# Feed-forward weight-quarter sums issued by GpSimd in tile order instead of by VectorE

## What is computed

```python
def swiglu_ffn(x, w_in, w_out):
    gate, up = jnp.split(x @ w_in, 2, axis=-1)
    return (jax.nn.silu(gate) * up) @ w_out

for i in range(DEPTH):            # DEPTH = 2, D_FF = 2816, D_MODEL = 1024
    x = x + 0.5 * swiglu_ffn(rmsnorm(x, norm_g[i, 0]), ffn_w_in[i, 0], ffn_w_out[i, 0])
    ...                           # pooling or convolution mixer
    x = x + 0.5 * swiglu_ffn(rmsnorm(x, norm_g[i, 2]), ffn_w_in[i, 1], ffn_w_out[i, 1])
```

## Time and profile before

| | |
|---|---|
| median of the runs | 2587.79 us |
| span of the profiled execution | 2585.3 us |
| TensorE matmul busy | 2552.6 us, 99% |
| VectorE busy | 1904.1 us, 74% |
| ScalarE busy | 1264.0 us, 49% |
| GpSimd busy | 191.5 us, 7% |
| mean granted TensorE clock | 0.997 |

### The profile page before, as it was taken

One profiled execution on the slowest core, in us unless ns is written; L12 is line 12 of the kernel. 1 busy time (PEld: TensorE's weight loads), 2 busy tenths in 40 slices (PEclk: granted clock), 3 DMA queues, 4 the chain that ended last, 5 costly groups with the idle time before them and its releaser, 6 DMA issues.

```text
span 2585.3 us, 43699 instructions
## 1 busy us (share of the span) xinstructions
PE 2552.6 (99%) x17223; PEld 2171.8 (84%) x17223; DVE 1904.1 (74%) x3109; ACT 1264.0 (49%) x2140; POOL 191.5 (7%) x248
## 2 busy tenths in 40 slices
PE   9999999999999989999999999999999999999999
PEld 7787878887777768999988999989999864889998
DVE  5765655686666678877769777688777698897775
ACT  5544445456665654444454444454444413444444
POOL 1110101013000010000020000010000421100000
PEclk9999999999999999999999999999999999999999
DMA  4222222122222212333322332223323472322232
GB/s 137 84 82 67 82 67 92 40 82 102 81 81 73 73 50 82 107 114 107 99 99 82 115 99 98 99 82 105 108 98 99 127 180 75 98 98 99 98 100 81
DMA packets 171883, 241.78 MB, mean 94 GB/s; under 512 B 6545, under 2 KB 149403, under 8 KB 171443
## 3 DMA queue, kind: packets, MB, share of 16 engines
q1 hardware_dynamic: 164755, 216.27, 25.7%
q0 software_dynamic: 6368, 21.79, 3.0%
q10 hardware_dynamic: 576, 1.16, 0.1%
HBM read 233.54 MB, written 5.58 MB: 92 GB/s over the span
## 4 chain that ended last, share of the span: by engine, by line
PE 88%; DVE 6%; ACT 2%; issue 2%; DMA 1%; POOL 0%; SPq 0%; POOLq 0%; DVEq 0%; ACTq 0%
PE ps L2000 8%; PE ps L2002 8%; PE ps L2001 8%; PE ps L440 5%; PE ps L442 5%; PE ps L441 5%; PE ps L2020 5%; PE ps L2021 5%; PE ps L2022 5%; PE ps L858 5%; PE ps L860 4%; PE ps L859 4%; PE ps L2748 1%; DMA w_raw<-in_ffn_w_out_dram 1%; DVE probs L1814 1%
## 5 line engine op out<-in xcount | busy, mean ns | idle before, releaser
L858 PE MATMUL ps<-h_hi,w_hi 128*128 128x512 f32 x608 | 255.2, 420 | 2.5 <-DVE w_lo L417 1.3
L2020 PE MATMUL ps<-a_hi,w_hi 128*128 128x512 f32 x640 | 250.2, 391 | 4.6 <-DVE a_lo L2315 4.6
L2122 ACT ACTIVATE wg<-w_raw 128x512 fp32r<-128x512 f32 x256 | 153.7, 624 | 197.7 <-PE ps L2002 98.0
L2021 PE MATMUL ps<-a_lo,w_hi 128*128 128x512 f32 x640 | 249.8, 390 | 0.0
L2022 PE MATMUL ps<-a_hi,w_lo 128*128 128x512 f32 x640 | 249.5, 390 | 0.0
L860 PE MATMUL ps<-h_hi,w_lo 128*128 128x512 f32 x608 | 237.9, 391 | 0.0
L859 PE MATMUL ps<-h_lo,w_hi 128*128 128x512 f32 x608 | 237.8, 391 | 0.0
L2000 PE MATMUL ps<-mix_late,wg 128*128 128x256 f32 x832 | 235.2, 283 | 0.1
L2002 PE MATMUL ps<-mix_late,wg 128*128 128x256 f32 x832 | 234.7, 282 | 0.0
L2001 PE MATMUL ps<-mix_late,wg 128*128 128x256 f32 x832 | 234.6, 282 | 0.0
L417 DVE TENSOR_TENSOR w_lo<-w_raw,w_hi 128x2048 fp32r<-128x2048 f32 x90 | 206.1, 2290 | 29.4 <-ACT w_hi L412 29.4
(11 more groups left out here) (463 smaller groups left out, 6614.4 us busy)
## 6 DMA issues: line engine op xcount, KB each, us to landing
w_raw<-in_ffn_w_in_dram SPq DMA_DIRECT2D x88, 1024.0 KB, 5.1
w_raw<-in_ffn_w_out_dram SPq DMA_DIRECT2D x44, 1024.0 KB, 4.9
w_raw<-in_a_w_in_dram SPq DMA_DIRECT2D x24, 1024.0 KB, 5.4
w_raw<-in_b_w_in_dram SPq DMA_DIRECT2D x16, 1024.0 KB, 5.4
w_raw<-in_conv_w_pw_dram SPq DMA_DIRECT2D x12, 1024.0 KB, 5.9
shifted<-glu_scratch POOLq DMA_DIRECT2D x32, 264.0 KB, 7.5
w_raw<-in_a_w_out_dram SPq DMA_DIRECT2D x8, 1024.0 KB, 4.9
w_raw<-in_b_w_out_dram SPq DMA_DIRECT2D x8, 1024.0 KB, 4.9
```

What stands on the lines that cost most here:

```text
L858: nc.tensor.matmul(dst, wh[:, w], h_hi[:, k], start=k == 0, stop=False)
L2020: nc.tensor.matmul(dst, wh[:, w], a_hi[:, buf, k], start=h == 0 and k == 0, stop=False, skip_group_check=h == 1)
L2021: nc.tensor.matmul(dst, wh[:, w], a_lo[:, buf, k], start=False, stop=False, skip_group_check=h == 1)
```

## The change

The four sums of every mixed gate and up tile are issued by GpSimd. `quarter_sum` calls `nc.gpsimd.tensor_tensor`, all its calls are taken out of `dve_steps` and `dve_ff`, and a new `gp_ff` issues them tile by tile, 5, 6, 7, 3 in each. `gp_ff` is called after `gp_sums` of each feed-forward's norm and first waits until the norm is broadcast, since the sums use its buffers. The sum of quarter 5 also waits for its own engine's earlier sum 6. Shapes, buffers and values are the same, and so is every other engine's order.

```diff
-        def quarter_sum(dve, f, s, u, *xs):
+        def quarter_sum(pool, f, s, u, *xs):
...
-            tt, t, i = nc.vector.tensor_tensor, step_tile(f, s, u), mixed_before(f, s, u)
+            tt, t, i = nc.gpsimd.tensor_tensor, step_tile(f, s, u), mixed_before(f, s, u)
             for x in xs:
                 if x == 5:
-                    dve.wait_ge(raw_loaded[t % 2], 16 * (t // 2 + 1))
-                    low_before(dve, f, s, u, 5)
+                    pool.wait_ge(raw_loaded[t % 2], 16 * (t // 2 + 1))
+                    low_before(pool, f, s, u, 5)
+                    if i:
+                        pool.wait_ge(mix_sum[6], i)
                     ins = tt(mix_s1, corner(t, 1, 0), corner(t, 1, 1), ALU.add)
                 elif x == 6:
-                    dve.wait_ge(mix_sum[5], i + 1)
-                    low_before(dve, f, s, u, 6)
+                    pool.wait_ge(mix_sum[5], i + 1)
+                    low_before(pool, f, s, u, 6)
                     if i:
-                        dve.wait_ge(mix_sum[3], i)
+                        pool.wait_ge(mix_sum[3], i)
                     ins = tt(mix_s2, mix_s1, corner(t, 0, 0), ALU.subtract)
                 elif x == 7:
-                    dve.wait_ge(mix_sum[5], i + 1)
+                    pool.wait_ge(mix_sum[5], i + 1)
                     ins = tt(corner(t, 1, 0), corner(t, 0, 0), corner(t, 1, 0), ALU.subtract)
                 else:
-                    dve.wait_ge(mix_sum[6], i + 1)
-                    dve.wait_ge(mix_lo, quarters_before(f, s, u, 2) + 1)
+                    pool.wait_ge(mix_sum[6], i + 1)
+                    pool.wait_ge(mix_lo, quarters_before(f, s, u, 2) + 1)
                     ins = tt(corner(t, 0, 1), corner(t, 0, 1), mix_s2, ALU.subtract)
                 ins.then_inc(mix_sum[x], 1)
+
+        def gp_ff(pool, f, m):
+
+            pool.wait_ge(bcast_ready, SPREAD.index(m) + 1)
+            for s in range(PLAIN, FF_STEPS):
+                for u in "gu":
+                    quarter_sum(pool, f, s, u, 5, 6, 7, 3)
...
         def dve_steps(dve, f, r):
             a, b = 2 * r + 1, 2 * r + 2
             add_pair(dve, f, r - 1, 5)
-            quarter_sum(dve, f, b, "g", 5)
             quarter_low(dve, f, a, "u", 2)
-            quarter_sum(dve, f, a, "u", 3)
-            quarter_sum(dve, f, b, "g", 6, 7)
...
             gp_sums(pool, 2)
+            gp_ff(pool, 0, 2)
             pool.wait_ge(band_stored, 16)
...
             gp_sums(pool, 4)
+            gp_ff(pool, 1, 4)
             gp_sums(pool, 5)
+            gp_ff(pool, 2, 5)
...
             gp_sums(pool, 8)
+            gp_ff(pool, 3, 8)
```

More of the change, by code:

```diff
@@ L2333, in add_pair, with low_before @@
                 nc.vector.scalar_tensor_tensor(xT[:, n], ps[:, 4 + n % 4], 0.5, xT[:, n], ALU.mult, ALU.add).then_inc(out_free, 1)
-        def low_before(dve, f, s, u, x):
+        def low_before(pool, f, s, u, x):
             i = mixed_before(f, s, u)
             if i:
-                dve.wait_ge(mix_lo, 7 * (i - 1) + MIX.index(x) + 1)
-        def quarter_sum(dve, f, s, u, *xs):
+                pool.wait_ge(mix_lo, 7 * (i - 1) + MIX.index(x) + 1)
+        def quarter_sum(pool, f, s, u, *xs):
@@ L2425, in dve_steps @@
             quarter_low(dve, f, b, "g", 5)
-            quarter_sum(dve, f, b, "u", 5, 7)
             quarter_low(dve, f, b, "g", 6, 2)
-            quarter_sum(dve, f, b, "g", 3)
             join(dve, f, a, "u", "c11")
-            quarter_sum(dve, f, b, "u", 6)
             quarter_low(dve, f, b, "g", 3)
@@ L2441, in dve_steps @@
             low_half(dve, f, a, 1)
-            quarter_sum(dve, f, b, "u", 3)
             join(dve, f, b, "g", "c11")
@@ L2456, in dve_steps @@
             low_half(dve, f, b, 0)
-            quarter_sum(dve, f, a + 2, "g", 5)
             low_half(dve, f, b, 1)
             quarter_low(dve, f, a + 2, "g", 1, 5)
-            quarter_sum(dve, f, a + 2, "g", 6)
             add_pair(dve, f, r, 0)
@@ L2465, in dve_steps @@
             add_pair(dve, f, r, 2)
-            quarter_sum(dve, f, a + 2, "g", 3)
             add_pair(dve, f, r, 3)
-            quarter_sum(dve, f, a + 2, "g", 7)
             quarter_low(dve, f, a + 2, "g", 3)
-            quarter_sum(dve, f, a + 2, "u", 5)
             quarter_low(dve, f, a + 2, "g", 7, 4)
             quarter_low(dve, f, a + 2, "u", 1, 5)
-            quarter_sum(dve, f, a + 2, "u", 6, 7)
             add_pair(dve, f, r, 4)
@@ L2506, in dve_ff @@
             hs_sum(dve, f, 6)
-            quarter_sum(dve, f, 2, "g", 5)
             ff_product(dve, f, 1, 1)
@@ L2512, in dve_ff @@
             add_first(dve, f, 1, 2)
-            quarter_sum(dve, f, 2, "g", 6)
             add_first(dve, f, 3)
@@ L2519, in dve_ff @@
             hs_low(dve, f, 3)
-            quarter_sum(dve, f, 2, "g", 3, 7)
             hs_low(dve, f, 7)
             quarter_low(dve, f, 2, "g", 3, 7, 4)
-            quarter_sum(dve, f, 2, "u", 5)
             quarter_low(dve, f, 2, "u", 1)
             join(dve, f, 2, "g", "c11")
-            quarter_sum(dve, f, 2, "u", 6)
             quarter_low(dve, f, 2, "u", 5)
@@ L2534, in dve_ff @@
             low_half(dve, f, 1, 1)
-            quarter_sum(dve, f, 2, "u", 3, 7)
             split_out(dve, f, 1)
@@ L2550, in dve_ff @@
             low_half(dve, f, 2, 1)
-            quarter_sum(dve, f, 3, "g", 5)
             quarter_low(dve, f, 3, "g", 1, 5)
             add_pair(dve, f, 0, 0, 1)
-            quarter_sum(dve, f, 3, "g", 6)
             add_pair(dve, f, 0, 2)
-            quarter_sum(dve, f, 3, "g", 7)
             add_pair(dve, f, 0, 3)
             quarter_low(dve, f, 3, "g", 6, 2)
-            quarter_sum(dve, f, 3, "g", 3)
-            quarter_sum(dve, f, 3, "u", 5, 6)
             quarter_low(dve, f, 3, "g", 3, 7, 4)
             quarter_low(dve, f, 3, "u", 1, 5, 6)
-            quarter_sum(dve, f, 3, "u", 7)
             add_pair(dve, f, 0, 4)
```

## The result

The changed kernel takes 2616.9 us in the median (2614.53 to 2618.84) against 2587.51 us of the kernel before in the same session: a ratio of 1.0112, with a 95% interval of 1.0098 to 1.0126. The forecast was 2610 us, so the direction and the range held, and the loss is 29 us where 22 were forecast. The profiled execution has a span of 2614.8 us, 29.5 more than before, at a mean granted clock of 0.998. Medians leave out two executions at a much lower granted clock, one with the spare additions (4214.78 us at 0.555) and one of the kernel before (3138.26 us at 0.751).

A forecast was written before the change was run, and what follows sets the result against it. TensorE, busy 99% of the span, was taken as the bound. Losses of 6 us at the starts, 14.4 in steady pairs and 2 for landing sums made 22.4 us, forecasting 2610 us with a range of 2589 to 2632.

The forecast's parts named there:

- What is at stake: Whole kernel: only TensorE's idle time can be won, about 5 us at most; VectorE's lead over TensorE is at risk.
- The hold-up of 1.05 us: VectorE operations with two SBUF inputs that meet a GpSimd sum right behind another such operation are delayed 1.05 us.
- Steady pairs: Steps 3 to 8, three pairs in each feed-forward: 1.2 us lost in each of 12, 14.4 us in all.
- the two meetings less one sum: End of a steady pair: next pair's sums delay VectorE around the low halves, 0.6 + 1.05 us, less 0.60.
- 1.5 of slack: Steady pairs: output tile b's `low_half` ends 1.5 us before TensorE starts its first chunk, absorbing that much delay.
- The start: Step 2 of each of four feed-forwards: VectorE's dense stretch lengthens by 1.5 us, 6 us in all.
- the landing sum: Step 2's pair: next tile's sum 5 lands just as `split_out` ends; half of 1.05 us each, 2 us in four.
- five less six sums: Start of a feed-forward: five hold-ups add 5.25 us, six sums leaving VectorE save 3.6, net 1.6, taken as 1.5.
- (a): Rival: only the start of each feed-forward loses, slack holds in steady pairs; 2594 to 2596 us, chance 0.15.
- (b): Rival: no change, step 2's hold-ups cost no more than the six sums saved; 2583 to 2593 us, chance 0.13.
- (c): Rival: faster, exclusion doesn't show and low parts stay at 0.69 us; 2583 or 2582 us, chance 0.04.
- (d): Rival: much slower, GpSimd's queue order pushes b-u's sums beyond 1209, each meeting costs 1.28 us; 2631 us, chance 0.16.

The follow-up runs named there:

- the spare additions: Kernel before, all sums on VectorE, plus 256 unused 128x512 additions on GpSimd in steps 3 to 10: 2756.17 us, ratio 1.0647.
- the fills: Changed kernel with each GpSimd sum replaced by two chained memsets that read nothing, sums left out: 2585.26 us, ratio 0.9989.
- step 2 alone: Kernel before with only the eight sums of step 2 in each feed-forward on GpSimd, 32 in all: 2596.81 us, ratio 1.0038.
- the later landing sum: Changed kernel, but GpSimd's sum 5 of the next pair's gate tile waits for the second low half of the pair before: 2596.67 us, ratio 1.0036.
- the low parts ahead of `split_out`: Kernel before, but step 2's low parts of up-tile quarters 3, 7, 4 precede the splitting of output tile 1 on VectorE: 2585.49 us, ratio 0.9991.
- both places mended: Changed kernel with step 2's sums on VectorE and GpSimd's next-pair sum 5 behind the second low half: 2589.51 us, ratio 1.0005.
- the spare fills: Kernel before plus, on GpSimd, two chained 128x512 fills without reads in place of each of 256 unused additions: 2588.91 us, ratio 1.0004.
- the short additions: Kernel before, sums on VectorE, plus 256 unused GpSimd additions of 128x64 instead of 128x512 elements: 2588.51 us, ratio 1.0002.
- step 2 on VectorE: Changed kernel, but the eight sums of step 2 in each feed-forward stay on VectorE: 2609.13 us, ratio 1.0076.
- the old order: Changed kernel with GpSimd's sums within a pair ordered closer to VectorE's old order, not tile by tile: 2625.15 us, ratio 1.0139.

## Why the prediction was right, and where it was off

**What is at stake** held. TensorE's idle time is all that counts; the fills, with VectorE's load taken off, gained about 3 us, and nothing gained more.

**The hold-up of 1.05 us** held, at 1.07 to 1.10 (L2290 2.32 for 1.22, low parts 1789 ns at most for 687, a low half 1.75 for 0.68), and so did GpSimd's getting in between two instructions in a row. The prediction also took from the Trainium skill ("SBUF — State Buffer", Who interferes with whom) an exclusion for the whole length of both instructions. The section's distinction between a GpSimd instruction that reads and one that only writes is borne out by the fills (688 ns). The whole length isn't: an addition of 0.32 us or more held a low part up by 0.13. And `split_out`, which the prediction had among the instructions that can be held up, never was: its 40 take 2.29 us as before.

**Steady pairs: 14.4 us forecast, 15.9 measured** as the growth of the twelve pairs by the starts of matmuls. 14.6 of it are the waits at L2020 by the gaps (1.11 to 1.39 each); the rest is mainly the matmul behind each wait, 0.08 us later than its usual place. Steps 9 and 10 had no wait, as forecast, but for 0.2 us in the second feed-forward. The terms stand too. The last low part of b-u was 1.67 us late for 1.55. Some of that was lost again ahead of `split_out` (1.23 late), and the two meetings less one sum were 1.27 for 1.05. The second `low_half` ends at 1239.39 - 5.57 = 1233.82, 2.50 us late where the prediction's terms make 2.60, and 1.5 of slack leave 1.0 of the 1.11 measured. Removing the two meetings alone removes all twelve waits: the 1.5 us of slack holds the rest.

**The start: 8 us forecast (6 + 2), 11.3 measured**, and this is the mis-sized term. By the starts of matmuls the first chunk of b is 2.86, 3.48, 2.92 and 2.08 us late in the four feed-forwards, where 2.0 was forecast for each. Both parts are too small. The stretch before the landing sum, read from the kernel with step 2 alone, is 1.78, 2.71, 1.85 and 1.85 instead of 1.5: 8.2 us instead of 6. Why the second feed-forward loses more is open. The landing sum makes the other 3.1 us instead of 2. It was taken at half a meeting, because the transfer was laid out to end just as `split_out` ends. In the first feed-forward the sum starts 1.26 us after `split_out` begins, waits, and takes its whole turn (1047.01 and 1047.96 above). In the fourth it starts at 2333.71, behind the start of the last `low_half` (2333.61), which it doesn't hold up, and costs least. The place of the stall was missed: the prediction had it at the low part of quarter 3 of "u", behind five meetings. There were four in the first feed-forward, the fifth fell in a wait of VectorE's, and the delay went another way, over output tile 1's transfer, ScalarE's high part of it and the copy queued behind it, to quarter 6 of "u". So it is partly luck that four meetings less the two sums ahead of that transfer came near what five less six sums had promised.

**The rest.** 11.3 + 15.9 + 0.2 = 27.4 us, which is what the mixed steps of the four feed-forwards grew by, of the 29.5 of the span. 0.6 us is spread over other stages, and 1.5 us lie in the pooling stage, which the change doesn't touch. TensorE runs there for 3 us at the lower clock:

```profile
1326.66:1329.65 2.99, 2.99 (x16) 2.99 (x15) 2.87 (x9) 2.68 (x9) 0.00 (x0) 0.50 0.00 0
```

Between the mixed steps of the first feed-forward and those of the second the changed kernel's trace has two such stretches, at 1326.3 and 1357.0 us, the kernel before's only one, at 1349.5. That part takes 85.0 to 85.1 us in this profiled execution and in those of step 2 alone, of the later landing sum, of the fills in place of the sums and of the low parts ahead of `split_out`, all with two, and 83.5 to 83.6 in those of the kernel before, of both places mended, of the spare fills and of the short additions, all with one. What decides it is open. The prediction's terms, 22.4 us, are short of the 27.4 by 5.

**The rivals.** (a) and (b) fall with the twelve steady waits, (c) with the low parts' 941 ns. (d)'s condition isn't met: the sums of b-u end at 1214.25 - 5.57 = 1208.7, as laid out, and of the two orders tried the tile order is the better.

## What to carry to other kernels

Two-input work with its inputs in SBUF, moved from VectorE to GpSimd, relieved nothing here while VectorE was in a dense stretch of the same kind of work: each 128x512 sum of 0.60 us that left came back as up to 1.1 us. Count the places where the receiving engine's instruction will fall on the short chain, and when its input lands, not the busy shares: two places made 27 of the 29 us here, and one wait that let the chain go first returned 20 of them. What only writes, or reads little (128x64), cost nothing on GpSimd here.

## What the runs showed of the hardware

- The hold-up fits the elements that GpSimd reads, not the length of its instruction: 0.13 us for 128x64, 1.10 for 128x512, nothing for a 128x512 fill of 0.53 us.
- A short wait of TensorE can cost more than itself. After six waits of 2.2 to 2.6 us, in the kernels with step 2 on VectorE and with the old order, the granted clock fell to the 1.2 GHz level for 3 us (0.50 in the stretch shown above), 1.6 us lost each time. The length of the wait alone doesn't decide it: with the spare additions the clock stayed full behind the wait that ends at 1120.92, 2.5 us by the gap. After the wait of 1.83 us in the changed kernel it didn't fall, as the stretch behind it shows:

```profile
1049.90:1053.00 3.10, 3.10 (x14) 2.55 (x15) 3.10 (x2) 1.16 (x2) 2.66 (x2) 1.00 0.89 309
```
